# Nine gate half tiles ahead of the softmax attention, and expert tokens in 32 chunks of 64 rows in place of 24 chunks of 128

## What is computed

```
h = rms_norm(x, norm1) * (1 + scale1) + shift1
z = h @ w_in                        # q, k, v of 16 heads, 6 forget logits, 3 x 1024 gate columns
o_sb, o_dil, o_fox = three causal token mixers (4 stick-breaking, 6 dilated, 6 forgetting heads)
merged = sum over branches of sigmoid(z_gate) * (o_branch @ w_branch)
x = x + gate1 * (merged @ w_o)
h2 = rms_norm(x, norm2) * (1 + scale2) + shift2
group = argmax(h2 @ w_rg + b_rg); two experts of that group's four by h2 @ w_re + b_re
y = sum over the two experts of gate * (silu(h2 @ w1[e]) * (h2 @ w3[e])) @ w2[e]     # 16 experts, width 256
x = x + gate2 * y; y_out = rms_norm(x, norm_f)
```

## Time and profile before

| what | us |
|---|---|
| median of 3 timed runs | 1507.87 |
| lowest and highest | 1503.69, 1515.48 |
| the profiled execution | 1507.89 |
| its span, first to last instruction | 1506.2 |
| PE busy in it | 1260.0 (84%) |
| DVE, ACT, POOL busy | 449.6, 296.0, 160.3 |
| mean granted clock of PE | 0.919 of full speed |

### The profile page before, as it was taken

How to read it: one execution, slowest core, us unless ns; L and a number is a source line. 1 busy time by engine, 2 the same in 40 slices (tenths; PEclk the granted TensorE clock), 3 DMA queues, 4 the chain that set the end, 5 groups by cost and what they waited for, 6 DMA issues and landing times.

```text
span 1506.2 us, 20059 instructions
## 1 busy us (share of the span) xinstructions
PE 1260.0 (84%) x6991; PEld 820.4 (54%) x6991; DVE 449.6 (30%) x1106; ACT 296.0 (20%) x613; POOL 160.3 (11%) x229
## 2 busy tenths in 40 slices
PE   4699999746999999976888888779994999999990
PEld 2277777423577777754555555557453444444440
DVE  4200000465222223224444444435344111111116
ACT  2200000232222222212222222213110111111112
POOL 0000000230011112210000000000000011111110
PEclk9799999878899999989989999979995899999995
DMA  8714332046355321069888898849013999999934
GB/s 308 282 65 159 115 111 101 24 146 221 112 197 198 141 86 58 1 231 314 287 279 260 292 302 294 299 167 321 14 42 114 355 319 319 312 313 316 306 120 178
DMA packets 152885, 304.23 MB, mean 202 GB/s; under 512 B 16030, under 2 KB 79287, under 8 KB 150192
## 3 DMA queue, kind: packets, MB, share of 16 engines
q1 hardware_dynamic: 142832, 277.10, 54.1%
q0 software_dynamic: 9408, 21.82, 4.0%
q10 hardware_dynamic: 576, 4.46, 0.9%
HBM read 283.37 MB, written 50.00 MB: 221 GB/s over the span
## 4 chain that ended last, share of the span: by engine, by line
PE 75%; DVE 10%; DMA 6%; issue 5%; SPq 2%; ACT 2%; POOL 0%; DVEq 0%; POOLq 0%; ACTq 0%
PE psum L847 65%; PE psum L1137 6%; DVE arena L1745 3%; DMA wring<-in_w_mod 2%; DMA hT<-gate_tiles 2%; PE psum L1401 1%; PE psum L1176 1%; DVE wring L1753 1%; DVE hT L2339 1%; PE psum L1058 1%; PE psum L976 1%; SPq L559 1%; DVE wring L1745 1%; DVE xT L2127 1%; SPq L563 1%
## 5 line engine op out<-in xcount | busy, mean ns | idle before, releaser
L847 PE MATMUL psum<-hT,wring 128*128 128x272 f32 x1280 | 304.2, 396 | 8.3 <-ACT hT L1458 8.3
L847 PEld LDWEIGHTS psum<-hT,wring 128*128 128x128 f32 x1280 | 241.4, 191 | 69.0 <-issue 20.8
L847 PE MATMUL psum<-arena 128*8 128x128 f32 (+6 forms) x1488 | 207.7, 338 | 6.5 <-DVE arena L1745 3.5
L847 PE MATMUL psum<-wring,hT 128*128 128x512 f32 x384 | 174.0, 607 | 17.4 <-DVE hT L2339 15.3
L847 PEld LDWEIGHTS psum<-arena 128*8 128x8 f32 (+5 forms) x1488 | 109.9, 119 | 92.0 <-issue 77.8
L847 PE MATMUL psum<-wring,arena 128*8 128x128 f32 (+3 forms) x1008 | 121.6, 425 | 16.7 <-DMA wring<-in_w_mod 10.5
L847 PEld LDWEIGHTS psum<-wring,hT 128*128 128x128 f32 x384 | 72.1, 193 | 105.3 <-issue 102.4
L847 PEld LDWEIGHTS psum<-wring,arena 128*8 128x8 f32 (+3 forms) x1008 | 52.3, 112 | 73.4 <-issue 61.1
L847 PE MATMUL psum<-arena,small 128*128 128x256 f32 (+8 forms) x162 | 50.4, 435 | 39.7 <-DVE arena L1745 27.7
L785 POOL TENSOR_SCALAR wring<-wring,arena 128x384 f32<-128x384 f32 (+6 forms) x32 | 45.6, 1425 | 282.4 <-DVE arena L2001 282.4
L733 DVE COPY arena<-psum 128x512 f32<-128x512 f32 x64 | 44.2, 691 | 98.7 <-PE psum L847 53.6
(11 more groups left out here) (235 smaller groups left out, 1207.5 us busy)
## 6 DMA issues: line engine op xcount, KB each, us to landing
wring<-in_w SPq DMA_DIRECT2D x48, 1024.0 KB, 11.2
arena<-in_cache_kv SPq DMA_DIRECT2D x128, 320.0 KB, 3.5
wring<-in_w_mod SPq DMA_DIRECT2D x12, 2048.0 KB, 13.0
arena<-in_w SPq DMA_DIRECT2D x24, 1024.0 KB, 5.1
xT<-in_cache_kv SPq DMA_DIRECT2D x64, 320.0 KB, 3.5
wring<-in_cache_kv SPq DMA_DIRECT2D x64, 320.0 KB, 3.5
out_dil_sample<-in_cache_dil SPq DMA_DIRECT2D x8, 2044.0 KB, 10.9
wring<-in_w_in SPq DMA_DIRECT2D x6, 2048.0 KB, 11.7
```

Of the source, the lines that this page charges most:

```text
L847: return T.matmul(out, lhsT, rhs, start=start, stop=stop, **k)
```

## The change

**Gates.** Half tiles 0 and 1 (`FIRST`) run on PE before the forget rows, half tiles 2 to 8 (`STICK`) in the four stick-breaking heads, two, two, two and one, between a head's following scores and its sum group. The other 39 are spread over the 32 softmax units, one or two in each. There is a fourth place for gate weights. SP loads chunk 0 of the weights as soon as the modulation is through, chunks 1 and 2 behind the stores of the sample rows (chunk 1 waits for the key stores, chunk 2 for the sample stores), and the copies of the window buffers now come behind these two. The stick-breaking outputs use one PSUM bank in place of two. The rows that hold the modulation's bias move, and DVE waits for their stores before the forget logits.

**Experts.** A chunk has 64 slots. Each expert has a first chunk (even chunks, 16), and 16 odd chunks take overflows: `OVER_AT` says which overflow stands at which odd chunk (0, 15, 1, 14, 2, 13 and so on). SP loads the first chunks' weights without registers, the first of them already while the rows of h2 are being made; POOL loads the overflows' weights by indirect DMAs (`over_weights`, four issues of 1 MB, 1 MB, 512 KB and 512 KB), with indices out of bounds, so that nothing is moved, where there is no overflow. There are four places for weights. w1 and w3 are read with 8 consecutive input rows in a partition, 8 KB, and the rows of h2 and the router's weights are put in the matching order. One gather fetches the rows of two chunks, of which each chunk turns its half. In `hidden` and `outputs` the 64 slots are the columns of the stationary side, and two matmuls, one for each half of the hidden units (or of the outputs), write PSUM partitions 0 to 63 and 64 to 127. The turns run two chunks ahead, and the loops are written out. DVE's slot arithmetic has more steps; ACT alone copies the turned rows and DVE alone the outputs. Scatters write half rows of 512, two for each pair.

```diff
-CHUNKS = NEXP + (TOP * TOK - NEXP) // P
+CROWS = 64
+OVER = 16
+CHUNKS = NEXP + OVER
+WSLOTS = 4
...
-        FILL = [(3 * n // 2 + n % 2,) if n % 2 == 0 else (3 * n // 2, 3 * n // 2 + 1) for n in range(NU)]
+        OVER_AT = [n // 2 if n % 2 == 0 else OVER - 1 - n // 2 for n in range(OVER)]
+        FIRST = (0, 1)
+        STICK = ((2, 3), (4, 5), (6, 7), (8,))
+        at = [9 + (39 * n) // NU for n in range(NU + 1)]
+        FILL = [tuple(range(at[n], at[n + 1])) for n in range(NU)]
...
+            sp.wait_ge(sem("w_used"), 12)
+            gate_weights(0)
             sp.wait_ge(sem("kt_ev"), 10)
             sp.wait_ge(sem("vt_ev"), 10)
...
+            sp.wait_ge(sem("st_k"), 16 * KV_STORES)
+            gate_weights(1)
+            sp.wait_ge(sem("st_smp"), 16 * SAMPLE_STORES)
+            gate_weights(2)
             for b in range(NB):
                 shift_copy(0, b)
                 shift_copy(1, b)
...
+            def base_weights(e):
+
+                slot = 2 * e % WSLOTS
+                if e >= 2:
+                    sp.wait_ge(sem("h_mm"), 2 * (e - 2) + 1)
+                for n, name in enumerate(("w1", "w3")):
+                    sp.dma_start(w13_at[slot][:, n, :], I[name][0, e].rearrange("(p k) f -> p (k f)", p=P)
+                                 ).then_inc(sem(f"ld_e{slot}"), 16)
+                if e >= 2:
+                    sp.wait_ge(sem("y_mm"), 2 * (e - 2) + 1)
+                sp.dma_start(w2_at[slot], I["w2"][0, e].rearrange("(k p) f -> p k f", p=P)
+                             ).then_inc(sem(f"ld_e{slot}"), 16)
...
+            def over_weights(c):
+
+                slot, j = c % WSLOTS, OVER_AT[c // 2]
+                if c >= WSLOTS:
+                    pool.wait_ge(sem("h_mm"), c - WSLOTS + 1)
+                    pool.wait_ge(sem("y_mm"), c - WSLOTS + 1)
+                    settle()
+                for n, name in enumerate(("w1", "w3")):
+                    pool.indirect_dma_start(
+                        out=w13_at[slot][:, n, :], out_offset=None,
+                        in_=I[name][0].rearrange("e (p k) f -> (e p) (k f)", p=P),
+                        in_offset=bass.IndirectOffsetOnAxis(ap=w13_i[:, j:j + 1], axis=0),
+                        bounds_check=NEXP * P - 1, oob_is_err=False).then_inc(sem(f"ld_e{slot}"), 16)
...
             settle()
-            for c in range(CHUNKS + RING):
-                if c < CHUNKS:
-                    gather(c)
-                if c >= RING:
-                    scatter(c - RING)
+            gather(0)
+            over_weights(1)
+            for m in range(1, RING):
+                gather(m)
+            over_weights(3)
+            for c in range(CHUNKS):
+                scatter(c)
+                if c % 2 == 0 and c // 2 + RING < CHUNKS // 2:
+                    gather(c // 2 + RING)
+                if c % 2 and c + WSLOTS < CHUNKS:
+                    over_weights(c + WSLOTS)
...
+            for u in FIRST:
+                gate_unit(u)
...
+                for n, u in enumerate(STICK[h]):
+                    if n:
+                        pe.wait_ge(sem("sbo_ev"), h)
+                    gate_unit(u)
                 pe.wait_ge(sem("sbsp"), h + 1)
...
+            def hidden(c):
+                slot = c % WSLOTS
+                pe.wait_ge(sem("xg_ev"), c + 1)
+                pe.wait_ge(sem(f"ld_e{slot}"), (64 if c % 2 else 48) * (c // WSLOTS + 1))
+                if c >= 2:
+                    pe.wait_ge(sem("hid_ready"), c - 1)
                 for k in range(KD):
-                    last = mm(banks[2 + slot], xg[:, slot, 128 * k:128 * k + 128],
-                              wring[:, slot, 512 * k:512 * k + 512], k == 0, k == KD - 1)
+                    for side in range(2):
+                        f0 = DE * k + P * side
+                        last = mm(banks[2 + c % 2][CROWS * side:CROWS * side + CROWS, 0:256],
+                                  xg[:, c % RING, CROWS * k:CROWS * k + CROWS], w13_at[slot][:, :, f0:f0 + P],
+                                  k == 0, k == KD - 1, skip_group_check=True)
                 last.then_inc(sem("h_mm"), 1)
...
+            for c in range(CHUNKS):
+                hidden(c)
+                if c:
+                    outputs(c - 1)
+                if c + 2 < CHUNKS:
+                    turn_rows(c + 2)
+                turn_hidden(c)
+            outputs(CHUNKS - 1)
```

More of the change, by code:

```diff
@@ L1538, in _ @@
                     stick_logs(h + 1)
+                for u in STICK[h]:
+                    gate_out(u)
                 for n, kt in enumerate((3, 2, 1, 0)):
@@ L1735, in _ @@
+            features_out(0)
+            features_out(1)
+            for c in range(CHUNKS):
+                gate_half(c)
+                if c + 2 < CHUNKS:
+                    features_out(c + 2)
+                hidden_out(c)
             A.preload_act_table_set("natural_log_exp_and_others")
```

416 lines of the change are left out of this document (193 added, 223 removed).

## The result

| | median, us | lowest to highest | runs |
|---|---|---|---|
| before | 1506.18 | 1503.69 to 1515.48 | 4 |
| after | 1468.7 | 1455.11 to 1474.09 | 4 |

What follows compares the result with a forecast made beforehand. PE bounds the softmax stretch; in the expert stage PE and DMA are both close to full. 1507.9 - 29.7 (gates) - 51.6 (experts) + 3.1 (routing) = 1429.7, so 1430 us; own range 1414 to 1450, with rivals 1398 to 1476.

Steps and rivals of the forecast that it cites:

- GpSimd rival: Expert stage: GpSimd's issuing of scatters, gathers and loads sets the pace, 17.5 us per two chunks; 1462 us, chance 0.14.
- the whole early part: Half tiles moved before the forget rows and into the stick-breaking heads: together +3.6 us, bounds -6 and +13.
- the filled stretch: Softmax attention where PE never waits: nine gate half tiles leave it, -33.3 us.
- "gates bring nothing" rival: Gate half tiles: early fillings all late (+13) and half of the 33.3 us lost; 1454 us, chance 0.06.
- +6.8 and +2.5: Stick-breaking head 1: late gate weights delay its sum group by 6.8 us, and the lower clock after idling costs some 2.5.
- some 11 us: Expert chunks: draining the array at four mode changes, 0.2 us each, would lengthen the first 24 chunks by this in all.
- 7.5 + 12.2 - 15.9 = 3.8 us: Expert stage: PE's stall for one real overflow in four chunks, issue delay plus transfer less the time until PE wants it.
- the 12.2 us: Expert stage: time to move 4.7 MB, being overflow weights, a base expert's down weights and a gather.
- first term: Expert stage: 7.5 us from a hidden layer's end through outputs, scatter and first load's issue to the first byte.
- 26 + 4.6: Start of the expert stage: 26 us for the first four chunks, 4.6 for the cold start.
- 73 - 2: Last eight expert chunks: 4 x 18.3 = 73 us for late pairs, 2 less at the end for half-length outputs.
- Routing: DVE's slot arithmetic, extra pickings and larger table and payload before the experts: +3.1 us, bounds 2 and 5.

Runs made afterwards that it cites:

- both, with the start mended: Changed kernel plus SP's loads waiting for the overflow, w1 and w3 issued early, gathers first and chunk 1's gate weights amid sample stores: 1438.7 us, ratio 0.953.

## Why the prediction was right, and what was mis-sized

**The number, and luck in it.** 1468.7 us lies in the range of 1398 to 1476, but outside the forecast's own range of 1414 to 1450. It is nearest to the time of the GpSimd rival (1462), for whose sake the range reached that far; yet this rival's mechanism did not occur, since with all the issues and none of the bytes the stage took 211.0 us. So the direction and the mechanisms were right, and that the range holds the result is in part luck.

**Gates: right, by its steps.** Hidden ahead of the forget rows; head 0 hidden; head 1 at 343.4 for 343.6; the whole early part +3.9 for +3.6; the filled stretch -32.8 for -33.3. The kernels with and without the early half tiles differ by 0.020 of the time, some 31 us, for -29.7. PE got the gate weights of head 1 at 334.25 (forecast about 336). The "gates bring nothing" rival (1454 us) is out. The 10 us of head 1's late weights could be had by another place in SP's order, which the prediction named as the spot (+6.8 and +2.5).

**PE's side of the experts: right.** Hidden layer 3.67 for 3.45, chunk 6.22 for 6.5, thus 0.3 us less than forecast. The waits stand before real overflow chunks only, as forecast, but not before all of them: chunks 27 and 31 have none, and chunk 1 none of its own. (The prediction's "some 11 us" for changes of mode kept the 2.9 us between two hidden layers as they were; with 0.8 more there too it would have been 7. Nothing of either is seen.)

**The step that failed** is the term "7.5 + 12.2 - 15.9 = 3.8 us" for the stall of a real overflow, and in it the 12.2 us; the seven stalls were 8.5 us on the mean. That counted what POOL and SP bring *for* the chunks at hand: the overflow, the w2 of a first chunk and a gather, 4.7 MB. It left out that SP's queue does not wait for POOL's: chunk 14's three loads stand in it around chunk 13's issue, and chunk 16's two behind it, and these take their share of the same engines. Over the transit to chunk 13 the engines moved 8.0 MB at 406 GB/s, 3.9 of them for SP, where the sum had 4.7 at 387: the rate was no worse, the bytes were. By the first term's end (the end of POOL's first issue) the forecast had 13.1 us to the landing, with the first byte. The trace has 19.7 (chunk 13), and for chunks 5, 9, 17 and 21 18.8 (1181.08 to 1199.84), 16.8 (1218.71 to 1235.52), 16.0 (1291.33 to 1307.36) and 16.4 (1325.40 to 1341.80). With chunk 16's loads held back it is 13.9, for 5.8 MB. The 0.9 us of the first byte, an estimate in the prediction, no row here shows by itself. The other two figures held: from the end of the hidden layer to the end of the first issue it took 6.7 us (1246.9 to 1253.6; forecast 6.6), and the window was 15.2 in place of 15.9, since a chunk is shorter.

The sum over the stage closes on this. From chunk 4's hidden layer (1183.26) to chunk 24's (1361.86) it is 178.6 us, 35.7 for four chunks; the forecast had 29.8, and 149 in all. Of the 5.9 us too much, the stalls make 5.3 (they average 9.07 in these five), the slower matmuls behind them 1.7, a cost that the prediction put at nothing, and the shorter chunks (4 x 0.28) take 1.1 off. Five times 5.9 is 29.6. The start cost 3.4 us more: 34.0 us from the first turn of rows to chunk 4 (forecast 26 + 4.6), since PE waited 4.68 us for the second gather, which stands behind chunk 1's loads in POOL's queue. The last eight chunks took 69.4 us, 1.6 less than forecast (73 - 2); but the forecast had them bound by bytes at 387 GB/s, and the trace has 320 GB/s there, two stalls (8.19 and 6.00) and PE's own pace between, so that this term is close by luck. Together 31.4 us: the stage is 282.0 in place of 250.6.

**Routing:** +2.2 for +3.1, within its bounds.

**What no step had:** the sequences' stretch, from the first cache page turned to the branch merge, took 352.4 us before and 360.6 after. It need not be the change: the kernels tried here have the same code there and show 352.4 (loads held back) to 361.0 us, with values between. In these stretches PE's granted clock is 0.85 to 0.89, 0.85 or 0.86 in three of the four longest; but the very longest (both, with the start mended, 361.0) had 0.88, so that the clock is not the whole of it:

```profile
628.00:988.00 360.00, 289.04 (x2984) 195.38 (x2984) 151.91 (x477) 84.62 (x171) 26.82 (x39) 0.85 0.82 273
```

```profile
654.00:1013.00 359.00, 285.62 (x2984) 191.33 (x2983) 152.02 (x480) 84.56 (x171) 26.77 (x39) 0.85 0.83 274
```

```profile
628.00:980.00 352.00, 275.74 (x2983) 185.62 (x2981) 151.91 (x480) 84.45 (x171) 26.79 (x39) 0.89 0.84 279
```

(After; the experts alone; loads held back.) The kernel with the experts alone, whose gates are as before, is among the long ones too. Why an execution is long or short there stays open. It puts some 8 us of chance on any single run: without it the profiled gain would be 46 us, near the ratio's 44.

**What stays open** in the experts: how much of the 20 us between loads on both queues, held back and early (261), and one queue (242) is the order and how much the idle time that the holding back itself makes. The first has engines busy 0.87 to 0.91 of the time in the two stretches from 1200 to 1300 us, the second 0.95 to 0.99; no kernel separates the two. Some 2.4 us of the 20 lie at the start, where PE waits 2.40 us before chunk 1 in place of 4.8. The 21 us from there to the plain loads on SP (221) are as open: both keep the engines busy, but at 378 and 415 GB/s, and why POOL's queue moves less is not shown.

## What to carry to other kernels

When loads are issued from two queues, a load's transit is not its own bytes over the rate: count what the other queue has in flight or will issue before it lands, above all loads for later steps. Put loads that are wanted in an order into one queue in that order, even where that gives the slower issuer more to do; here it was worth more (282 to 242 us for the stage) than issuing the late one earlier (8.6 us) or in a cheaper form (2 us, nothing by the stage's noise). And when a matmul engine waits some microseconds, price the wait with the slower matmuls behind it, as the granted clock falls in it: here 1.8 us on top of each wait of 8.5.

## What the runs showed of the hardware

- Two fp32 matmuls with 64 stationary columns, writing PSUM partitions 0 to 63 and 64 to 127, run side by side: 32 records of 256 columns in 3.67 us, where as many columns over 128 stationary ones took 7.13. Alternating with full-width turns in every chunk cost no time that the sum shows.
- Loads with 8 KB in a partition's row (w1, w3) and 4 KB (w2), in order on SP's queue, with gathers and scatters on POOL's beside them, kept the DMA engines at 415 GB/s for 150 us (1200 to 1350 us of that kernel; 387 with the rows of 2 KB).
- One queue issued by GpSimd, plain and indirect loads mixed, kept 378 GB/s over 50 us with the engines 0.99 busy.
- With both queues full the DMA engines kept 406 to 416 GB/s and served both: SP's loads, all for later chunks, took 48% of their time between POOL's first issue for chunk 13 and the end of PE's wait.
- GpSimd needs 1.3 us from one indirect load's issue to the next, whether it moves 1 MB, 512 KB or nothing (1192.70 to 1194.04 and 1290.30 to 1291.64 us, empty and full), and none of it bounds this stage: without the bytes it takes 211 us.
